# Sliding attention's two key blocks in one 128x128 probability tile per head, spread after the transpose by masked copies on VectorE

## What is computed

```python
def swa_mixer(q, k, v, positions, qn_w, kn_w, sinks):
    ...                                    # q, k normed and rotated
    kw = with_prev_block(k...)             # keys: block before and own block, 2 x 128
    vw = with_prev_block(v...)
    s = jnp.einsum('bnqkgd,bnckd->bkgnqc', qb, kw)
    diff = qpos[:, :, None] - kpos[:, None, :]
    mask = (diff >= 0) & (diff < SWA_WINDOW) & (kpos[:, None, :] >= 0)     # SWA_WINDOW = 128
    s = jnp.where(mask, s, -jnp.inf)
    m = jnp.maximum(jnp.max(s, axis=-1, keepdims=True), sink)
    p = jnp.exp(s - m)
    denom = jnp.sum(p, axis=-1, keepdims=True) + jnp.exp(sink - m)
    o = jnp.einsum('bkgnqc,bnckd->bkgnqd', p, vw) / denom
```

## Time and profile before

| | us |
|---|---|
| timed runs, median (lowest to highest) | 1577.01 (1576.83 to 1578.54) |
| profiled execution | 1578.62 |
| its span, first to last instruction | 1576.8 |
| TensorE busy (granted clock 0.999 of full speed) | 1557.1 |
| VectorE busy | 1041.3 |
| ScalarE busy | 771.5 |

### The profile page before, as it was taken

One profiled execution on the slowest core, in us unless ns is written; L12 is line 12 of the kernel. 1 busy time (PEld: TensorE's weight loads), 2 busy tenths in 40 slices (PEclk: granted clock), 3 DMA queues, 4 the chain that ended last, 5 costly groups with the idle time before them and its releaser, 6 DMA issues.

```text
span 1576.8 us, 21326 instructions
## 1 busy us (share of the span) xinstructions
PE 1557.1 (99%) x7488; PEld 1275.3 (81%) x7488; DVE 1041.3 (66%) x1487; ACT 771.5 (49%) x1163; POOL 106.9 (7%) x92
## 2 busy tenths in 40 slices
PE   8999999999999999999999999999999999999998
PEld 7877778888778888888788787788887888888886
DVE  5677664554776657586866767655457676665778
ACT  5657552222556464546445566422235563636362
POOL 0000000000121010111000000000002111101010
PEclk9999999999999999999999999999999999999999
DMA  7321324532596655747323212155317856666553
GB/s 235 103 81 57 96 64 147 173 107 81 132 222 140 177 137 151 170 110 208 55 86 102 81 55 80 54 173 174 107 54 157 236 115 177 144 175 134 145 122 94
DMA packets 132363, 201.48 MB, mean 128 GB/s; under 512 B 6625, under 2 KB 82977, under 8 KB 132257
## 3 DMA queue, kind: packets, MB, share of 16 engines
q1 hardware_dynamic: 107600, 153.37, 29.3%
q0 software_dynamic: 23936, 46.14, 17.6%
q10 hardware_dynamic: 720, 0.61, 0.1%
HBM read 170.74 MB, written 2.10 MB: 110 GB/s over the span
## 4 chain that ended last, share of the span: by engine, by line
PE 87%; DVE 9%; DVEq 2%; issue 1%; ACT 1%; DMA 0%; ACTq 0%
PE acc L593 19%; PE acc L595 19%; PE acc L594 19%; PE acc L656 6%; PE acc L657 6%; PE acc L658 6%; DVE wl_rows L1196 3%; PE acc L615 3%; PE acc L617 2%; PE acc L616 2%; DVE x_tokens L1561 1%; PE bank L793 1%; PE bank L812 1%; PE bank L804 1%; DVE ul L1215 1%
## 5 line engine op out<-in xcount | busy, mean ns | idle before, releaser
L593 PE MATMUL acc<-uh,wh 128*128 128x512 f32 x1152 | 453.5, 394 | 1.6 <-DVEq L1217 1.2
L595 PE MATMUL acc<-uh,wl 128*128 128x512 f32 x1152 | 449.3, 390 | 0.0
L594 PE MATMUL acc<-ul,wh 128*128 128x512 f32 x1152 | 449.2, 390 | 0.0
L593 PEld LDWEIGHTS acc<-uh,wh 128*128 128x128 f32 x1152 | 216.4, 188 | 53.9 <-issue 6.0
L595 PEld LDWEIGHTS acc<-uh,wl 128*128 128x128 f32 x1152 | 216.4, 188 | 45.3
L594 PEld LDWEIGHTS acc<-ul,wh 128*128 128x128 f32 x1152 | 216.6, 188 | 43.4
L1196 DVE TENSOR_TENSOR wl<-raw,wh 128x1024 fp32r<-128x1024 f32 x142 | 174.0, 1226 | 103.6 <-ACT wh L888 91.9
L888 ACT ACTIVATE wh<-raw 128x1024 fp32r<-128x1024 f32 x142 | 150.6, 1060 | 141.0 <-PE acc L595 88.8
L888 ACT ACTIVATE wh_rows<-raw_down 128x1024 fp32r<-128x1024 f32 x140 | 148.5, 1061 | 131.6 <-PE acc L658 101.9
L1196 DVE TENSOR_TENSOR wl_rows<-raw_down,wh_rows 128x1024 fp32r<-128x1024 f32 x140 | 171.5, 1225 | 26.0 <-ACT wh_rows L888 13.4
L1060 ACT ACTIVATE gate_tanh<-gate_tanh 128x512 f32<-128x512 f32 x40 | 25.3, 633 | 164.5 <-DVEq L1227 164.5
(11 more groups left out here) (257 smaller groups left out, 2443.0 us busy)
## 6 DMA issues: line engine op xcount, KB each, us to landing
raw<-in_w_in_dram SPq DMA_DIRECT2D x39, 1024.0 KB, 5.2
raw<-in_w_up_dram SPq DMA_DIRECT2D x32, 1024.0 KB, 6.3
raw_down<-in_w_down_dram SPq DMA_DIRECT2D x32, 1024.0 KB, 8.8
raw_down<-raw_down POOLq DMA_DIRECT2D x44, 512.0 KB, 5.5
raw_down<-in_w_down_dram POOLq DMA_DIRECT2D x32, 512.0 KB, 6.3
raw_branch<-in_w_in_dram SPq DMA_DIRECT2D x12, 1024.0 KB, 5.0
raw_branch<-in_w_branch_dram SPq DMA_DIRECT2D x12, 1024.0 KB, 5.0
raw_down<-in_w_o_dram SPq DMA_DIRECT2D x8, 1024.0 KB, 8.2
```

The costliest lines, as they stand in the source:

```text
L593: nc.tensor.matmul(a[:], wh[slot][:, k, :], right_h, start=at_k == 0, stop=False)
L594: nc.tensor.matmul(a[:], wh[slot][:, k, :], right_l, start=False, stop=False)
L595: last = nc.tensor.matmul(a[:], wl[slot][:, k, :], right_h, start=False, stop=at_k == n - 1)
```

## The change

The mask is no longer added to 256 columns. For i not 0 or 4, VectorE copies the own block's scores of a head pair, then copies the block before over them where the column is past the row (the mask's bits serve as predicate). The probability tile is 128 wide per head; exponential, sum and scaling run over 128 columns. TensorE turns 4 tiles for every i, into one bank. VectorE, no longer ScalarE, takes the turned tile to `probs_keys`: by one masked copy per block, into places that ScalarE sets to zero once a layer (`ptz`). The steps PTi leave ScalarE's order and enter VectorE's, and PVi waits once. The masks come in one transfer, 128x384 words in place of 128x128, and the constants lose 128 columns.

```diff
 DVE_ORDER (the steps added; nothing else moves)
-... SC0 +cx0 SM0 SC1 KV0 SM1 +cx1 KV1 PV0 +cx2
-gr0 SC2 ... OS YG0 ... cx3 +cc3 SC4 ...
-... YT1 cc3 SC6 ... SM6 cv0 +gate0 YT3 ct1 SC7 cl0 ct2 SM7 PV5 cv1 cv2
-+gate1 +gate2 cl1 ct3 +gate3 PV6 cv3 cl2 ...
+... SC0 +cx0 SM0 SC1 KV0 SM1 PT0 +cx1 KV1 PV0 +cx2
+gr0 PT1 SC2 ... OS PT2 YG0 ... cx3 +cc3 PT3 SC4 ...
+... YT1 PT4 cc3 SC6 ... SM6 cv0 PT5 +gate0 YT3 ct1 SC7 cl0 ct2 SM7 PT6 PV5 cv1 cv2
++gate1 +gate2 cl1 ct3 +gate3 PV6 PT7 cv3 cl2 ...
@@ TensorE
                     elif kind == "PT":
                         pe.wait_ge(probs_ready, l * 8 + i + 1)
-                        for cur in ((0, 1) if i % TT else (1,)):
-                            b = open_bank(l, word + ("cur" if cur else "prev"))
-                            for h in range(4):
-                                last = nc.tensor.transpose(b[:, h * P:(h + 1) * P], sm[i % 2][:, h, cur * P:(cur + 1) * P], ident)
-                            last.then_inc(bank_full, 1)
+                        b = open_bank(l, word)
+                        for h in range(4):
+                            last = nc.tensor.transpose(b[:, h * P:(h + 1) * P], sm[i % 2][:, h, :], ident)
+                        last.then_inc(bank_full, 1)
...
+                        pe.wait_ge(probs_T_ready, l * 8 + i + 1)
                         if n:
-                            pe.wait_ge(pprev_ready, l * 6 + half * 3 + n)
                             for kv in range(SWA_KV):
                                 weighted(kv, 0)
-                        pe.wait_ge(pcur_ready, l * 8 + i + 1)
@@ ScalarE
-                    elif kind == "PT":
-                        for cur in ((0, 1) if i % TT else (1,)):
-                            b, free = filled(l, word + ("cur" if cur else "prev"))
-                            nc.scalar.activation(pT[:, cur].rearrange("p h c -> p (h c)"), b[:], ACT.Copy).then_inc(free, 1)
-                            nc.scalar.drain().then_inc(pcur_ready if cur else pprev_ready, 1)
+                    elif kind == "ptz":
+                        nc.scalar.activation(pT[:].rearrange("p c h n -> p (c h) n"),
+                                             zero_col.unsqueeze(2).broadcast_to([P, 2 * 4, P]), ACT.Copy).then_inc(probs_T_zero, 1)
@@ VectorE
                         for odd in range(2):
                             b, free = filled(l, word + "ab"[odd])
-                            V.tensor_tensor(sm[buf][:, 2 * odd:2 * odd + 2, first:],
-                                            b[:].rearrange("p (j c) -> p j c", j=2)[:, :, first:],
-                                            swam.unsqueeze(1).broadcast_to([P, 2, 2 * P])[:, :, first:], ALU.add).then_inc(free, 1)
+                            to, keys = sm[buf][:, 2 * odd:2 * odd + 2, :], b[:].rearrange("p (j c) -> p j c", j=2)
+                            if i % TT:
+                                V.tensor_copy(to, keys[:, :, P:])
+                                V.drain()
+                                V.copy_predicated(to, in_block_before.unsqueeze(1).broadcast_to([P, 2, P]),
+                                                  keys[:, :, 0:P]).then_inc(free, 1)
+                            else:
+                                V.tensor_tensor(to, keys[:, :, P:], swam.unsqueeze(1).broadcast_to([P, 2, P]),
+                                                ALU.add).then_inc(free, 1)
...
+                    elif kind == "PT":
+                        b, free = filled(l, word)
+                        dve.wait_ge(probs_T_zero, l + 1)
+                        for cur in ((0, 1) if i % TT else (1,)):
+                            last = V.copy_predicated(pT[:, cur], keys_of[:, cur].unsqueeze(1).broadcast_to([P, 4, P]),
+                                                     b[:].rearrange("p (h n) -> p h n", h=4))
+                        last.then_inc(free, 1)
+                        V.drain().then_inc(probs_T_ready, 1)
```

More of the change, by code:

```diff
@@ L83 @@
 PE_FIRST = "gq0.0 gq1.0 gq0.1 gq1.1 gk0 gk1.0 UT0 NROW gk1.1".split()
[L86 to L90, removed]
+ACT_ORDER = """+gk1 UT0 UT1 ss0 UT2 UT3 ss1 ss2 ss3 +kva0 +kva1 attz +kva2 +kva3 +sq0 +sq1 +sq2 kva0 kva1 kva2 kva3 ptz +sq3 +gv0 ZA +gv1
++gv2 sq0 sq1 sq2 sq3 ZB +gv3 KT0 +gr0 +gr1 +gr2 gv0 gv1 KT1 gv2 KD +gr3 gv3 QT0 QT1 QT2 QT3 +cx0 SC0 SM0 SC1 +cx1
+SM1 PV0 +cx2 gr0 gr1 gr2 SC2 gr3 +cx3 GO0 SC3 SM2 GO1 +cc0 SM3 PV1 mz1 +cc1 mz2 mz0 mz3 PV2 +cc2 +cc3 SC4
++cb0 YT0 PV3 SM4 +cb1 SC5 +cb2 SM5 YT1 +cb3 YT2 PV4 SC6 +gate0 YT3 SM6 cb0 PV5 +gate1 SC7 +gate2 SM7 cb1
+cb2 +gate3 PV6 +br0 cb3 gate0 PV7 +br1 gate1 +br2 gate2 gate3""".split()
 DVE_ORDER = """+gk1 UT0 UT1 UT2 UT3 RN +kva0 NROW gk0 +kva1 +kva2 gk1 +kva3 +sq0 +sq1 +sq2 kva0 kva1 kva2 kva3 +sq3 AT +gv0 ZA ZB
[L94 to L97, removed]
++gv1 sq0 sq1 sq2 sq3 +gv2 X0 +gv3 QS +gr0 QM +gr1 X1 QR +gr2 ATT0 +gr3 ATT1 SC0 +cx0 SM0 SC1 KV0 SM1 PT0 +cx1 KV1 PV0 +cx2
+gr0 PT1 SC2 gr1 gr2 SC3 gr3 +cx3 SM2 GO0 SM3 cx0 GO1 OS PT2 YG0 cx1 YG1 +cc0 +cc1 cx2 +cc2 PV1 PV2 cx3 +cc3 PT3 SC4 cc0 ct0 SM4
+SC5 +cb0 YT0 +cb1 cc1 PV3 SM5 cc2 +cb2 YT1 PT4 cc3 SC6 +cb3 YT2 PV4 SM6 cv0 PT5 +gate0 YT3 ct1 SC7 cl0 ct2 SM7 PT6 PV5 cv1 cv2
++gate1 +gate2 cl1 ct3 +gate3 PV6 PT7 cv3 cl2 +br0 cl3 gate0 PV7 gate1 +br1 gate2 +br2 gate3""".split()
 PE_LATE = """wo0 wo1 wo2 wo3 wo4 wo5 wo6 wo7 wo8 wo9 wo10 wo11 wo12 V0 V1 V2 V3 wo13 up0.0 V4 V5 V6 V7 up1.0 up2.0 up3.0 up0.1
@@ L211 @@
 CC = dict(ident=0, invf=128, ones=136, scan=137, swam=649)
-N_CONST = 905
+N_CONST = 777
 HEADS_Q = SWA_HEADS + SWA_KV
@@ L276, in hybrid_trunk @@
         attm = at("gla_att", 76, [GLA_HEADS, TT, P])
-        sm = [at(f"probs{i}", 80 + 2 * i, [4, 2 * P]) for i in range(2)]
+        sm = [at(f"probs{i}", 80 + 2 * i, [4, P]) for i in range(2)]
         gt = at("gate_tanh", 80, [4, SEQ])
@@ L312, in hybrid_trunk @@
         cst = after("consts", [N_CONST])
-        gm = after("gla_mask", [P], i32)
+        masks = after("masks", [3, P], i32)
+        gm, keys_of = masks[:, 0], masks[:, 1:]
         par = after("params", [N_PARAMS])
@@ L340, in hybrid_trunk @@
         scanm = cst[:, CC["scan"]:CC["scan"] + SEQ]
-        swam = cst[:, CC["swam"]:CC["swam"] + 2 * P]
+        swam = cst[:, CC["swam"]:CC["swam"] + P]
+        in_block_before = swam.bitcast(i32)
         neg4, d4, sum4, es4, den4 = ([small[:, 8 * i + 4 * j:8 * i + 4 * j + 4] for j in range(2)] for i in range(5))
@@ L863, in _ @@
                 act.dma_start(xc[:, k, :], x_cols[k * P:(k + 1) * P]).then_inc(xc_full[k], 16)
-            act.dma_start(gm[:], gmask).then_inc(gm_full, 16)
+            act.dma_start(masks[:].rearrange("p c n -> p (c n)"), gmask).then_inc(gm_full, 16)
             def filled(l, name):
@@ L1711, in constants @@
     c[:, CC["scan"]:CC["scan"] + SEQ] = np.arange(SEQ) % GLA_CHUNK != 0
-    key = np.arange(2 * P)[None, :]
-    c[:, CC["swam"]:CC["swam"] + 2 * P] = np.where((key > p[:, None]) & (key <= p[:, None] + P), 0.0, -3.0e38)
+    c[:, CC["swam"]:CC["swam"] + P] = np.where(p[None, :] <= p[:, None], 0.0, -3.0e38)
     freq = np.float32(500000.0) ** (-np.arange(0, 2 * half, 2, dtype=np.float32) / np.float32(2 * half))
@@ L1716, in constants @@
     g = (p[None, :] >= p[:, None]) & (p[None, :] // GLA_CHUNK == p[:, None] // GLA_CHUNK)
-    return c, g.astype(np.int32)
+    return c, np.concatenate([g, p[None, :] < p[:, None], p[None, :] >= p[:, None]], axis=1).astype(np.int32)
 def kernel(**inputs):
```

24 lines of the change are left out of this document (10 added, 14 removed).

## The result

| | median, us | lowest to highest | runs |
|---|---|---|---|
| before | 1577.27 | 1576.72 to 1579.05 | 10 |
| after | 1581.18 | 1580.58 to 1582.69 | 10 |
| profiled execution, before / after | 1578.62 / 1582.43 | span 1576.8 / 1580.6 | 1 each |

The ratio is 1.0022, with a 95% interval of 1.0014 to 1.0030. The changed kernel is slower by 0.2%. The forecast was 1576.3 us with a range up to 1581.0, so the time lies just above the range. Three later executions (2468 and 3986 us of the kernel before, 6261 us in the first of experiments 7 and 8) stand far off: the ratios leave them out, and they move no median by more than 0.1 us.

The account below looks back on a forecast made before the run. TensorE, busy 99% of the span, bounds the kernel. Removing 5.2 us of transposes, less waits at PV0, SC3 and PV7 and 0.2 us at the start, gives -0.7 us against 1577.01: 1576.3 us, range 1573.4 to 1581.0.

Parts of the forecast that it names:

- TensorE's side: Attention stage: six PT steps a layer turn 4 tiles instead of 8, 0.43 us each, 5.2 us removed over two layers.
- VectorE's side: PT steps on VectorE cost 1.6 us with two masked copies, 0.94 with one; the SC step changes by -0.1 to +0.3.
- The second rival: Masked steps cost more and VectorE paces the attention stage; loss begins at a 1.7 us PT step, 1580.2 to 1585; chance 0.12.
- The waits in their places: TensorE waits for VectorE in each layer's attention stage: 0.1 us at PV0, 0.45 at SC3, 1.6 at PV7.
- SC3: Scores whose bank VectorE's last masked copy of PT1 frees: start at 127.15 us in layer 0, a new wait of 0.45 us.
- PV7: Last weighted sums of each layer: PT7 is ready at 226.65 us in layer 0, so TensorE waits 1.6 us.
- the sum: Per layer -2.6 + 0.1 + 0.45 + 1.6 = -0.45 us; two layers -0.9, start +0.2, so -0.7.
- The stated warning: The prediction is wrong altogether if other places, such as the start or the projections, move by over 1 us.
- The start: Kernel start: the mask's transfer grows from 64 to 192 KB, costing 0.2 us, between 0 and 0.4.
- The masked steps cost more, and VectorE paces the stage: Attention stage: dearer masked copies add up on VectorE ahead of PV7, giving 1580.2 to 1585 us; chance 0.12.
- PV3, YT1 or the linear attention's output: Places in the attention stage where a TensorE pause would show that the masked steps cost more and VectorE paces the stage.
- Gain and waits cancel, or miss by a little: TensorE's queue gets shorter but it stands longer, costs towards the upper bound: 1578 to 1580.2 us; chance 0.15.

Follow-up runs that it names:

- experiments 7 and 8: Changed kernel with PV7's wait filled, then with tiles 1 and 7 turned early; both with 18 throw-away transposes misplaced at `mixed_diff`: 1581.95 and 1577.95 us.
- experiment 3: Changed kernel without masks behind the transpose: ScalarE copies each turned tile whole twice, VectorE has no PT step, order of before; 1576.60 us, ratio 0.9983.
- experiment 5: Changed kernel with 12 throw-away transposes on TensorE during PV7's wait, nothing made earlier; 1578.85 us, ratio 1.0003 to the kernel before.
- 9: The changed kernel once more, unaltered, on the same chip as the fills; 1581.17 us, ratio 1.0018 to the kernel before.

## Why the prediction was wrong

**TensorE's side was right.** 48 tiles at 0.43 us per four were to give 2.6 us a layer. In experiment 3, where nothing waits, starts move ahead by 0.43 to 0.47 us at each of the six steps.

**VectorE's side was right.** The pair of masked copies took 1.33 to 1.37 us in the timeline in all twelve places, forecast 1.40; one over 256 columns 449 ns, forecast 473; the copy 421 ns, as the addition of that shape in the earlier trace rows. The second rival, masked steps above 1.7 us, had no part. PV6 and PT7 in layer 0:

```profile
223.99 0.86 DVE L1518 TENSOR_TENSOR yl<-bank,yh 64x256 fp32r<-64x256 f32 x2 [0.25 <-issue]
225.10 1.33 DVE L1507 COPY_PREDICATED probs_keys<-masks,bank 128x512 f32<-128x512 int32 x2 [0.25 <-issue]
```

**The waits in their places were right.** SC3 came at 127.22 us with a wait of 0.44 (forecast 127.15, 0.45), PV7 at 226.62 with 1.50 (226.65, 1.6), to be held against the earlier trace rows. Layer 1 was a little dearer: 0.55 and 1.80 us. With the clock at its upper level throughout, as in the run with filled waits, layer 0's stage gained about 0.6 us and layer 1's 0.3, against the 0.45 each of the sum.

**The step that failed is the price of a wait in the sum.** It put PV7's wait at its own length, no term stood for the clock behind a wait, PV7's or any other, and the difference was set against 1577.01 us, the level at which the kernel before has no half-clock stretch. The lengths were right, but TensorE then ran its next matmuls at half clock in some executions, 1.6 us each time. The difference between the changed kernel and the same kernel with its waits filled, on one chip, is 3.8 us of the 4.9 us by which the forecast was low, and by the traces some 3.2 us of it are such stretches.

How they divide between PV7 and the `mixed_s` waits, which both kernels have, isn't settled. Filling PV7's alone gave 2.3 us (experiment 5 against 9, on two chips), with the groups of times of the kernel before again, around 1577.2, 1578.7 and 1580.2. That is more than the one stretch that layer 1's wait can bring, for layer 0's (1.40 to 1.50 us) was never followed by one. In the three traces that keep layer 1's wait (1.78 to 1.80 us) with no fill, it was followed once, and the `mixed_s` waits five times out of six; in the other traces with a `mixed_s` wait of 2.3 us or more, eight times out of twelve. So most of the loss may stand behind waits that the change didn't make, and why they are followed by half clock in none, one or both layers of the kernel before, and in both layers in both traces of the changed one, is open. No run fills the `mixed_s` waits alone, or any wait of the kernel before. The stated warning, other places moving by over 1 us, did occur: at 434 us by 1.6.

**The other 1.1 us** is mostly the three pauses of VectorE, 0.36 + 0.34 + 0.27 us in the run with filled waits. The prediction read pauses marked as issue only as a part of each step; that some stand at fixed places in the instruction list, and move with any edit, it did not have. The start cost nothing where the sum had 0.2 us: at 36 us the changed kernel is 0.1 us later than the kernel before in its first trace and 0.2 us earlier with the waits filled.

**The rivals.** None of them was this one. "The masked steps cost more, and VectorE paces the stage" gave 1580.2 to 1585 us, which holds the measured time, but by luck: it rested on PT steps above 1.7 us and on pauses at PV3, YT1 or the linear attention's output, and the steps took their 1.6 us and no new pause stood at those places. "Gain and waits cancel, or miss by a little" (1578 to 1580.2 us) rested on costs towards the upper bound, which did not occur either.

The Trainium skill (TensorE: Matmul & The Clock Gate, "What's actually happening") says that the array's clock is set at half or full rate by how busy the engine has lately been, and that the moment of switching isn't tied to the kernel's start, so that the same kernel differs from run to run. This case's traces agree: two waits of 2.33 us in one execution, with 1.00 behind one and 0.59 behind the other.

## What to carry to other kernels

In this kernel a wait of TensorE of 1.8 us or more could cost its length and 1.6 us on top; look at the granted clock behind each long wait, in several executions, and count the groups in the timed runs. Where the wait can't be removed, throw-away transposes into the tile about to be overwritten kept the clock, provided that they stood at the step that waits, ahead of its semaphores; elsewhere they only cost time. Better is the step moved ahead: one word of VectorE's order turned a loss of 0.2% into a gain of 0.1%, and a second word with the filled `mixed_s` wait made it 0.3%.

## What the runs showed of the hardware

- **Waits and half clock.** In the 14 traces, from 20 us on, TensorE has 19 waits of 2.03 to 2.70 us, and 14 are followed by the lower clock; 7 of 1.78 to 1.85 us, of which 3 are; and 34 of 1.07 to 1.54 us, of which none is. The lower level began between 0.5 us before and 1.3 us after TensorE's next start, lasted 3.4 us and cost about 1.6 us each time.
- **Filling a wait** with 128x128 transposes at 0.12 us each (12 in 1.47 us, 18 in 2.13 us) kept the clock at its upper level behind all four filled waits of a trace, and behind all twelve in five traces, and made eleven executions agree within 0.7 us.
- **Pauses of VectorE by place.** Pauses of 0.42 to 0.47 us with nothing that releases them moved to other steps when 24 idle instructions were put at the start; all 92 in the 14 traces stand 63 records past a multiple of 128. The Trainium skill (Runtime: NRT & Kernel Launch, "Instruction fetch mechanics") says that an engine's instructions are refilled in blocks of 256 while it runs, mostly hidden. The spacing of 128 records is half such a block, and no run here shows whether these pauses are refills; that they go with the place in the list is what was shown.
